# One group of side work after every row block, the two lanes in turn

## What is computed

```python
def first_block(x, mem, ...):
    # layer A: mLSTM with four heads of 256, and attention to a memory of 256 tokens
    h = rmsnorm(x, norm_g)
    qk, v, o, z, i_pre, f_pre, mq, mz = split_cols(h @ w_in, ...)
    qk = jax.nn.silu(causal_conv(qk, conv_w, conv_b))      # width-4 convolution over time
    ht = rmsnorm(mlstm_chunkwise(q, k, v, i_pre + ig_b, f_pre + fg_b), h_g)
    y_m = jax.nn.sigmoid(o) * ht * jax.nn.silu(z)
    x = x + concat([y_m, memory_attention(mq, mz, mk, mv)]) @ w_out
    # layer B: latent attention, eight heads, chunk-causal, and the memory again
    k_sh, v_sh = shared_kv(x, ...)
    x = x + concat([attn * silu(z), memory_attention(...)]) @ w_out

def second_block(x, mem, ...):
    # pooling and differential attention (four heads), cross attention to a second memory, MLP
    x = x + (concat([y_pool, y_attn]) * gates) @ w_out
    x = x + memory_cross_attention(...)
    x = x + jnp.square(jax.nn.relu(hm @ w_up)) @ w_down
    return rms_norm(x, g_final)
```

## Time and profile before

| | us |
|---|---|
| median of 3 runs | 1846.99 (1843.93 to 1851.82) |
| the profiled execution, its own time | 1849.4 |
| its span, first to last instruction | 1847.6 |
| PE busy in the span | 1668.5 (90%) |
| DVE, ACT busy | 890.8 (48%), 750.9 (41%) |
| mean granted TensorE clock | 0.938 of full |

### The profile page before, as it was taken

How to read it: one execution, slowest core, us unless ns; L and a number is a source line. 1 busy time by engine, 2 the same in 40 slices (tenths; PEclk the granted TensorE clock), 3 DMA queues, 4 the chain that set the end, 5 groups by cost and what they waited for, 6 DMA issues and landing times.

```text
span 1847.6 us, 19774 instructions
## 1 busy us (share of the span) xinstructions
PE 1668.5 (90%) x7336; PEld 1293.1 (70%) x7336; DVE 890.8 (48%) x1879; ACT 750.9 (41%) x1714; POOL 66.3 (4%) x64
## 2 busy tenths in 40 slices
PE   6993898999899986877988999887999999999997
PEld 4761576878677874655766888455778778888886
DVE  4357436556346354445543446744555344444343
ACT  5352323232335454556542333433433343334343
POOL 0001001010100000000000000000000000000000
PEclk9995999999899997888999999868999999999999
DMA  5320122222324220111211332102333223332232
GB/s 198 92 69 0 46 72 66 61 88 77 118 69 129 60 66 17 48 36 42 64 68 46 104 92 85 41 1 69 93 101 103 87 96 102 93 102 92 91 103 80
DMA packets 85120, 141.54 MB, mean 77 GB/s; under 512 B 7200, under 2 KB 32160, under 8 KB 85024
## 3 DMA queue, kind: packets, MB, share of 16 engines
q1 hardware_dynamic: 83728, 137.45, 24.1%
q10 hardware_dynamic: 1296, 2.83, 0.4%
HBM read 138.17 MB, written 2.10 MB: 76 GB/s over the span
## 4 chain that ended last, share of the span: by engine, by line
PE 78%; DVE 10%; ACT 7%; issue 2%; DMA 1%; POOL 1%; ACTq 0%; DVEq 0%; POOLq 0%
PE banks L1059 13%; PE banks L1060 13%; PE banks L1061 13%; PE banks L1054 8%; PE banks L1056 8%; PE banks L1055 8%; PE banks L1019 3%; DVE sb_arena L1711 2%; PE banks L1146 1%; ACT sb_arena L1484 1%; DVE sb_w_split L1711 1%; DVE sb_arena L1720 1%; PE banks L1243 1%; PE banks L1227 1%; ACT sb_junk L1318 1%
## 5 line engine op out<-in xcount | busy, mean ns | idle before, releaser
L1711 DVE TENSOR_TENSOR sb_w_split<-sb_raw,sb_w_split 128x512 fp32r<-128x512 f32 (+4 forms) x520 | 323.5, 664 | 351.2 <-ACT sb_w_split L1355 350.0
L1355 ACT ACTIVATE sb_w_split<-sb_raw 128x512 fp32r<-128x512 f32 (+4 forms) x520 | 286.3, 600 | 271.9 <-PE banks L1061 133.5
L1059 PE MATMUL banks<-sb_w_split,sb_actB 128*128 128x512 f32 (+2 forms) x752 | 304.4, 405 | 18.7 <-DVE sb_actB L1720 7.9
L1060 PE MATMUL banks<-sb_w_split,sb_actB 128*128 128x512 f32 (+2 forms) x752 | 296.0, 394 | 0.0
L1061 PE MATMUL banks<-sb_w_split,sb_actB 128*128 128x512 f32 (+2 forms) x752 | 295.0, 392 | 0.0
L1054 PE MATMUL banks<-sb_actA,sb_w_split 128*128 128x512 f32 x672 | 270.3, 402 | 2.5 <-DVE sb_arena L1720 1.5
L1056 PE MATMUL banks<-sb_actA,sb_w_split 128*128 128x512 f32 x672 | 262.3, 390 | 0.0
L1055 PE MATMUL banks<-sb_actA,sb_w_split 128*128 128x512 f32 x672 | 262.0, 390 | 0.0
L1019 PE MATMUL banks<-sb_cons,sb_arena 128*128 128x128 f32 x508 | 100.5, 310 | 105.1 <-DVE sb_arena L1714 61.7
L1059 PEld LDWEIGHTS banks<-sb_w_split,sb_actB 128*128 128x128 f32 x752 | 146.7, 195 | 49.1 <-DVE sb_actB L1720 9.2
L1059 PE MATMUL banks<-sb_w_split,sb_actA 128*128 128x512 f32 (+1 forms) x416 | 166.4, 400 | 2.5 <-DVE sb_arena L1720 1.5
(11 more groups left out here) (163 smaller groups left out, 1889.8 us busy)
## 6 DMA issues: line engine op xcount, KB each, us to landing
sb_raw<-in_a_w_in SPq DMA_DIRECT2D x64, 256.0 KB, 3.0
sb_raw<-in_w_up SPq DMA_DIRECT2D x32, 512.0 KB, 3.6
sb_raw<-in_w_down SPq DMA_DIRECT2D x32, 512.0 KB, 3.7
sb_raw<-in_w_in SPq DMA_DIRECT2D x24, 512.0 KB, 3.6
sb_raw<-in_mem_w_kv SPq DMA_DIRECT2D x16, 512.0 KB, 4.1
sb_raw<-in_a_w_in SPq DMA_DIRECT2D x16, 512.0 KB, 3.6
sb_raw<-in_w_ckv SPq DMA_DIRECT2D x16, 512.0 KB, 3.7
sb_raw<-in_a_w_out SPq DMA_DIRECT2D x12, 512.0 KB, 3.7
```

What stands on the lines that cost most here:

```text
L1059: pe.op.matmul(out, x.hi(k)[:, cs], hi, start=i == 0, stop=False)
L1060: pe.op.matmul(out, x.hi(k)[:, cs], lo, start=False, stop=False)
L1355: act.op.activation(hi[:, cs], raw[:, cs], ACT.Copy).then_inc(act.mark(m("w_hi"), 2 * n + part + 1), 1)
L1711: dve.op.tensor_tensor(out, a, b, op).then_inc(dve.mark(*mark) if mark else dve.tick(), 1)
```

## The change

`Plan.step` advances one lane instead of both, lane 1 first and then in turn (`turn`), and still takes one entry of `soon`. `Plan.product` calls it after every row block instead of after every chunk. A lane thus still gets one group for two row blocks, while `soon` gets one entry for each row block; the step behind a product's evictions now advances one lane alone; and in `Plan.need` each step brings one lane's group instead of both. No instruction is added or taken away.

```diff
+        self.turn = 0
@@ Plan.step
         if self.soon:
             for step in self.soon.popleft():
                 self.put(step)
-        for lane in (1, 0):
-            self.advance(lane)
+        self.turn = 1 - self.turn
+        self.advance(self.turn)
@@ Plan.product
-            for _ in range(kk):
+            for inner in range(kk):
                 ahead = ks[min(i + SRC_LEAD.get(pr.src, 0), len(ks) - 1)]
                 self.need(source_step(pr.src, ks[i]), source_step(pr.src, ahead))
                 banks = ...
                 self.put(("mm", name, i), banks)
                 i += 1
-            if i == len(ks):
+                if i == len(ks):
...
-            else:
-                self.counts["chunk"] += 1
-                self.chunk_place.append(("chunk", 0, self.counts["chunk"]))
-            self.step()
+                elif inner == kk - 1:
+                    self.counts["chunk"] += 1
+                    self.chunk_place.append(("chunk", 0, self.counts["chunk"]))
+                self.step()
```

More of the change, by code:

```diff
@@ L343, in product @@
                 i += 1
-            if i == len(ks):
[L345 to L354, removed]
-            else:
-                self.counts["chunk"] += 1
-                self.chunk_place.append(("chunk", 0, self.counts["chunk"]))
-            self.step()
+                if i == len(ks):
+                    last = n_out(name) - 1
+                    place = self.place[("mm", name, 0), last]
+                    self.chunk_place.append(("full", place.bank, place.turn))
+                    self.need(*before_ev)
+                    for j in range(n_out(name)):
+                        self.put(("ev", name, j))
+                        if pr.ev == "res":
+                            self.put(("rsq", name, j))
+                        if soon is not None:
+                            self.soon.extend(soon(j))
+                elif inner == kk - 1:
+                    self.counts["chunk"] += 1
+                    self.chunk_place.append(("chunk", 0, self.counts["chunk"]))
+                self.step()
     def finish(self):
```

## The result

The changed kernel took 1857.25 us (median; 1854.35 to 1861.09) where the kernel before took 1848.08 in the same runs: a ratio of 1.0049, 95% interval 1.0026 to 1.0072. It is slower by half a per cent, 9 us, and 22 us above the 1835.2 that was forecast. The profiled execution of the changed kernel took 1861.1 us, with a span of 1859.3, 3.8 over its median; so the traces differ by 11.7 us where the medians differ by 9.2.

A forecast was written before the change was run, and what follows sets the result against it. PE, busy in 1668.5 of 1847.6 us, was taken as the bound, so only its idle time, some 179 us, counted. Terms summed to -11.8 us, from 1846.99 to 1835.2 us; range 1818 to 1849.

The forecast's parts named there:

- Part 1: Heads 1 and 3: csilu comes earlier, so hsc no longer waits for POOL's multiplies; -19.6 us.
- Part 2: Heads 1 to 3: hrs behind a displaced convolution, its scalings held up by POOL, so hty waits; +15.6 us (+6.9 to +18.3).
- First burst: Before ozA0: DVE meets hnr's root on POOL with little left to do; +1.5 us (-2 to +3).
- Memory attention of B: kvB0's first row block covers the values product's wait of 2.37; -2.4 us (-5 to 0).
- Preparation bursts: Head preparation before kvB1, kvB2 and kvB3: reordered steps shorten PE's waits; -6.6 us (-10 to 0).
- Burst before outC0: pw.3 moves ahead of gC0's last row block and cuts the wait of 2.95; -1.5 us (-2.9 to 0).
- ckD0: Squares for the second memory's norm come one row block later, so the wait of 2.41 grows; +1.5 us (0 to 2).
- Insertions cost nothing: Within products: twice as many insertions leave PE no idle time, so they cost nothing.
- B: Rival: gain given back, every scaling behind a multiply, layer B's bursts bound by ACT and DVE; 1846.9 us, chance 0.25.
- A: Rival, heads: DVE isn't held up by the multiplies and hty waits 2.3; 1826.5 us, chance 0.20.
- C: Rival, layer B's score groups: cover is halved, a lane's stage one short row block from its use; 1877 us, chance 0.07.

The follow-up runs named there:

- e_mult: Changed kernel with csilu's multiplies of heads 1 to 3 cut to 8 columns, work left out; only its trace is read: heads' stage 16.2 us shorter.
- e_warm: Changed kernel with 20 extra matmuls on PE ahead of hty's wait in heads 0, 1 and 2; ratio 1.0028 to the kernel before.
- e_silu: Changed kernel with the two silu steps of each product zB put together; 1850.7 us, ratio 1.0014 to the kernel before.
- e_lanes: Kernel before with lanes in turn behind every row block, convolutions and csilu at the old pace; 1856.1 us, ratio 1.0040.
- e_bburst: Changed kernel with a group of each lane at each step of layer B's bursts; 1873.8 us, ratio 1.0143 to the kernel before.
- e_soonlast: e_soon with `soon` taken behind the lanes, not ahead; 1832.3 us, ratio 0.9905 to the kernel before.
- e_soon: Kernel before with one entry of `soon` per row block, lanes at their old pace and place; 1848.9 against 1849.5 us, ratio 1.0001.
- e_hrs: Changed kernel with the lane's group ahead of `soon` at each turn; 1841.9 us, ratio 0.9954 to the kernel before.
- e_best: e_soonlast with entries other than conv, csilu and silu put ahead of the lanes again; 1828.6 us against 1846.7 for the kernel before, ratio 0.9892.

## Why the prediction was wrong

- **Part 1** (-19.6): right, to 0.1 us.
- **Part 2** (+15.6): the mechanism was right, its size not. The waits were 14.6 us in all where 13.8 had been taken, and e_mult splits each as the prediction did, 1.8 to 2.0 for the convolution (it had 2.2 or 2.3) and 3.0 for the hold-up. The Trainium skill (SBUF — State Buffer, "Who interferes with whom") states that a DVE instruction in a two-port mode and a GpSimd instruction shut each other out for the whole instruction, and that a `tensor_scalar` can enter such a mode; 4.15 us with the multiplies and 1.14 without agree, though no run shows the mode. The term that failed is the clock: 0.6 us for each wait, called scaled to the wait's length from the earlier trace rows. It was 2.2 by e_warm. The 0.6 isn't what that scaling gives: 1.9 and 3.1 us behind waits of 7.3 make 1.2 and 2.0 behind one of 4.6, which would have put 1.8 to 4.1 us more into the sum. Nor does the length of a wait settle its clock: the waits of 7.3 us had 1.9 and 3.1 us behind them, those of 4.9 have 2.2, those of 2.0 in e_mult none; the one of 1.85 at the start of outB0 has a granted clock of 0.87 behind it in the changed kernel, and the same wait (1.84) in e_silu 1.00. What else it hangs on was not tried. By the three stretches this part is 22.1 us and eats part 1 by itself.
- **First burst** (+1.5): the order was read rightly, and the end of the range (+3.1) was the value. The step that failed is "the other work of DVE there covers under 1 us of it": it covered next to none of the root. The longest wait grew by 3.0; smaller ones shrank by 1.8, among them the 0.83 at the end, and PE was busy 2.4 us longer, most of it slow clock, so that the stretch from qkA0 to the start of vA0 grew by 3.6. Another 1.6 us of the stage lie ahead of qkA0; four experiments with the changed kernel's order there have +0.2, +0.9, +1.1 and +3.2, so this is scatter between traces.
- **Memory attention of B** (-2.4): right, -2.6.
- **Preparation bursts** (-6.6): wrong in sign, +3.2 (+0.6 to +0.9 in e_mult, e_warm and e_lanes), the largest single miss. Two steps failed. The first is "prep4 no longer waits, prep6 still waits for DVE behind an exponential, and 8.4 us are left": 11.6 were left. prep4 did come free, but I had not counted all that stands ahead of prep6 on ACT: a second exponential with its table load came ahead of it, where the kernel before has one, between the two silus. From zB1 to zB2 and from zB2 to zB3, with the same 208 PE instructions each, the changed kernel takes 1.1 and 0.5 us more where 2.3 less was forecast for each. e_silu shows that ACT's loads lie on this chain, and e_bburst that the number of score groups doesn't set it; which of ACT's and DVE's other instructions made the 0.9 us over the kernel before is argued from the order, not tried. The second is a place that the sum did not have: prep3, moved ahead of the last row block, stands ahead of zB3's evictions too, which makes the wait of 1.85 at the start of outB0. (From zB0 to zB1 the changed kernel is 3.6 us shorter and from zB3 to outB1 5.1 longer; a score group of 8 PE instructions moved from the one to the other, so only the two together, +1.6, can be read, and 2.0 less had been forecast.) Every traced kernel that takes the lanes in turn has a wait there, and those at the old pace have none. The other bound, "0: the same engines do the same work", was no bound: an order can add to the chain.
- **Burst before outC0** (-1.5): +0.2 from gC0 to outC1, just outside the bounds (-2.9 to 0). The step that failed is that pw.3's place takes up to 2.72 off the wait of 2.95: pw.3 moved as read, and the wait is 2.96, as it is 2.94 in e_soonlast with pw.3 at its old place.
- **ckD0** (+1.5): +3.6. The wait grew by 0.43 and one of 0.98 was new, 1.4 us in all; the rest is slow clock, again the term that was left out.
- **Insertions cost nothing**: right.

Of the rivals, B ("given back in full", 1846.9) had the mechanism in both halves, hold-up without exception and bursts bound by ACT and DVE; it was still 10 us short, because its clock term was 0.9 for each wait, and because the bursts and the start of outB0 could get worse, which it did not allow. A is out by e_mult. C (halved cover, 1877) did not occur inside products, where the scores of layer B show no new wait; the wait of 3.44 us inside the bursts, one group behind its scores, fits its mechanism, which no run took apart. The range ended at 1849 because its cases charged the new waits of the heads with at most 0.9 us of clock and those elsewhere with none, and let no preparation burst get longer.

What stays open: what besides its length decides how much slow clock follows a wait, why mk1 to ckvB got 2.9 us shorter in e_soon, and how much of the 3.0 us at the first matmul of vA2 (e_hrs, e_soonlast, e_best) can be had back.

## What to carry to other kernels

Moving work forward to remove a wait puts it ahead of something else: list what it now precedes on each engine's queue, and whether it meets an engine that it holds up; here one swap of two lines turned a change worth nothing into one worth 1%. Charge a new wait of PE with the slow clock that can follow it, as a range: here it was 0 to 3.1 us, and the length of the wait alone did not settle it. In a stretch that one engine's chain sets, count that engine's switches between kinds of function, not only its work. And before reading 2 us from one stage of one trace, see how far that stage differs between traces of the same order.

## What the runs showed of the hardware

A wait of PE of 4.8 to 5.0 us cost 2.2 us beyond itself: the granted clock was 0.80 to 0.89 over the 16 to 17 us that contain it. The same wait filled with matmuls whose result nobody reads left the clock at 1.00. Four scalings of 128x256 on DVE took 1.14 us alone and 4.15 beside three multiplies of 128x512 on POOL, which took 3.80 there, 1.26 to 1.31 each (1.26 and 1.27 with DVE idle, at 316.44 and 317.66 in the kernel before), and so lost next to nothing; beside a convolution on DVE, in e_hrs, three took 4.69, 1.56 each on average. A table load on ACT took 1.28 us each time.
